# VectorE's masking of the forward diagonal score blocks, moved ahead of the last six operations of its pair

## The reference, cut to what matters

```python
p = p + (quad_shift(p, grid[0], grid[1]) - p) * mu
r, k, v, g, wl_f, wl_b, al_f, al_b = split_cols(p, RWKV_SIZES)
kk = to_heads(k * k_k, RWKV_HEADS).astype(jnp.float32)
kk = kk * lax.rsqrt(jnp.maximum(jnp.sum(jnp.square(kk), -1, keepdims=True), 1e-24))

def direction(w_lr, w0, ww2, a_lr, a0, wa2):
    w = jnp.exp(-RWKV_DECAY_SCALE * jax.nn.sigmoid((w0 + jnp.tanh(w_lr) @ ww2).astype(jnp.float32)))
    a = jax.nn.sigmoid(a0 + a_lr @ wa2)
    kh = to_heads(k * (1.0 + (a - 1.0) * k_a), RWKV_HEADS)
    bonus = jnp.sum(rh * kh * rk, -1, keepdims=True) * vh
    return (rh, to_heads(w, RWKV_HEADS), kh, vh, -kk, kk * ah), bonus
```

## Time and profile before

| | |
|---|---|
| median of 3 runs | 2932.02 us (2931.72 to 2933.52) |
| profiled execution, its span from first to last instruction | 2938.5 us |
| TensorE busy | 2522.4 us, 86% |
| VectorE busy | 1628.9 us, 55% |
| ScalarE, GpSimd busy | 918.9 us, 788.3 us |
| mean granted TensorE clock | 0.916 of full |

### The profile page before, as it was taken

The page is one execution under the profiler, slowest core; times in us unless marked ns, Lnnn a source line. Parts: engine busy times, 40 slices in busy tenths (PEclk is TensorE's granted clock), DMA queues, the critical chain, the costliest instruction groups (busy, mean ns, idle before and its releaser), DMA issues. The chain is left out here.

```text
span 2938.5 us, 56618 instructions
## 1 busy us (share of the span) xinstructions
PE 2522.4 (86%) x24270; PEld 2141.8 (73%) x24270; DVE 1628.9 (55%) x2534; ACT 918.9 (31%) x1488; POOL 788.3 (27%) x745
## 2 busy tenths in 40 slices
PE   6899898996898985676777999999689999996986
PEld 2577675675877874555566888878589999996765
DVE  3037787554356546685485566566546656564333
ACT  2113243231232334563203323333343334340310
POOL 1111111115756742111313222222122222121521
PEclk8899998998899997678898999999889999998998
DMA  7612445555343324120562444443634343412621
GB/s 267 239 52 84 136 134 145 149 154 162 86 112 95 95 76 117 25 73 17 174 147 76 154 164 156 165 163 141 226 120 164 117 159 109 158 58 71 204 90 60
DMA packets 338281, 374.11 MB, mean 127 GB/s; under 512 B 111279, under 2 KB 274742, under 8 KB 335470
## 3 DMA queue, kind: packets, MB, share of 16 engines
q1 hardware_dynamic: 337024, 367.15, 39.0%
q10 hardware_dynamic: 1006, 3.33, 0.3%
HBM read 230.60 MB, written 139.82 MB: 126 GB/s over the span
## 5 line engine op out<-in xcount | busy, mean ns | idle before, releaser
L3321 PE MATMUL PS<-V_hi,weights_hi 128*128 128x258 f32 x832 | 237.9, 286 | 10.4 <-DVE H L3532 6.9
L469 PE MATMUL PS<-hT_hi,w_in_hi 128*128 128x512 f32 (+1 forms) x640 | 239.5, 374 | 4.7 <-DVE q_out L3120 4.7
L469 PE MATMUL PS<-h_hi,w_in_hi 128*128 128x512 f32 (+1 forms) x624 | 233.1, 374 | 8.2 <-issue 4.6
L3322 PE MATMUL PS<-V_lo,weights_hi 128*128 128x258 f32 x832 | 236.8, 285 | 0.0
L471 PE MATMUL PS<-hT_hi,w_in_lo 128*128 128x512 f32 (+1 forms) x640 | 236.2, 369 | 0.0
L470 PE MATMUL PS<-hT_lo,w_in_hi 128*128 128x512 f32 (+1 forms) x640 | 236.1, 369 | 0.0
L3323 PE MATMUL PS<-V_hi,weights_lo 128*128 128x258 f32 x832 | 235.7, 283 | 0.0
L3429 POOL TENSOR_TENSOR weights_lo<-weights,weights_hi 128x1664 fp32r<-128x1664 f32 x32 | 122.0, 3812 | 412.4 <-ACT weights_hi L3381 412.4
L470 PE MATMUL PS<-h_lo,w_in_hi 128*128 128x512 f32 (+1 forms) x624 | 228.1, 366 | 0.0
L471 PE MATMUL PS<-h_hi,w_in_lo 128*128 128x512 f32 (+1 forms) x624 | 227.3, 364 | 0.0
L3293 PE MATMUL PS<-Q_hi,K_hi 128*128 128x256 f32 x640 | 184.2, 288 | 30.5 <-DMA K_lo<-kl_d 14.8
(11 more groups left out here) (462 smaller groups left out, 6378.3 us busy)
## 6 DMA issues: line engine op xcount, KB each, us to landing
chunk_in<-in_d SPq DMA_DIRECT2D x40, 512.0 KB, 3.5
w_in<-in_e_w_in_dram SPq DMA_DIRECT2D x30, 512.0 KB, 5.0
xnew<-in_o_w_in_dram SPq DMA_DIRECT2D x30, 512.0 KB, 6.2
in_d<-xnat SPq DMA_DIRECT2D x20, 640.0 KB, 6.1
modw<-in_mod_w_dram SPq DMA_DIRECT2D x12, 1024.0 KB, 9.5
xnat<-in_mod_w_dram SPq DMA_DIRECT2D x8, 1536.0 KB, 7.3
v_d<-xnew SPq DMA_DIRECT2D x16, 640.0 KB, 3.0
kh_d<-k_hi SPq DMA_DIRECT2D x16, 640.0 KB, 2.9
```

Source lines behind the costliest of these rows:

```text
L469: pe.matmul(PS[:, bank + off // 512, 0:n], wh[:, k], hh[:, k, t], start=(k == 0), stop=False)
L3321: pe.matmul(out, wh, VH[:, j, q], start=(j == seen[0]), stop=False)
L3322: pe.matmul(out, wh, VL[:, j, q], start=False, stop=False)
```

## The change

The call `blocks(p, 0)` moves from the end of VectorE's row for k = 4 to the place right behind L1067.

```diff
--- before.py
+++ after.py
@@ -1065,6 +1065,7 @@
                         dve.wait_ge(ready[1], 4 * p + 1)
                         link(dve.tensor_tensor(kk, kk, kt[1], ALU.mult))
                         dve.tensor_tensor(kk, kk, aa[1], ALU.mult).then_inc(ready[1], 1)
+                        blocks(p, 0)
                         dve.wait_ge(ready[1], 4 * p + 2)
                         link(dve.tensor_scalar(aa[1], aa[1], col(p, J_KA), ka1[:, p:p + 1], ALU.mult, ALU.add))
                         dve.tensor_tensor(aa[1], K, aa[1], ALU.mult).then_inc(s["kh_ok"], 1)
@@ -1074,7 +1075,6 @@
                         dve.wait_ge(ready[0], 4 * p + 4)
                         link(dve.tensor_tensor(khs, khs, aa[1], ALU.add))
                         dve.scalar_tensor_tensor(khs, R, col(p, J_RK), khs, ALU.mult, ALU.mult).then_inc(s["rk_ok"], 1)
-                        blocks(p, 0)
 
                 for n in range(last + 1):
                     prep(n)
```

## The result

The changed kernel takes **2909.64 us** (median of 4 runs, 2908.69 to 2915.1) against 2932.77 us for the kernel before (4 runs, 2931.72 to 2936.89): a ratio of 0.9921, 95% interval 0.9908 to 0.9934. That is 23.1 us less, where the prediction had 18.5 (2932.0 to 2913.5 us). The profiled execution after took 2909.42 us; its first to last instruction is a span of 2907.6 us, at a mean granted clock of 0.922.

What follows compares the result with a forecast made beforehand. TensorE was taken to bound the stage, stalled 18.0 us by late masks. Pairs 0, 1 and 2 give 4.5 + 10.4 + 3.6 = 18.5 us, so 2932.0 becomes 2913.5 us; range 2905.5 to 2924.5.

Steps and rivals of the forecast that it cites:

- three stalls: TensorE's waits before `w0` of pairs 1, 2 and 3, for the masks' PSUM banks: 4.45, 10.25 and 3.34 us, all to go.
- a gain of nothing: Rival, chance 0.09: block stores too slow, so pair 1 gives nothing and pairs 0 and 2 leave 8.1 us: 2923.9 us.
- no stop of 3.5 us was added: Rival, chance 0.08: three backward products each meet a 3.5 us stop and 3.1 us of low clock, no change: 2933 us.
- the rest of the program did not lengthen: Rival, chance 0.03: the shift of later work meets the clock's grants badly, costing 28.7 us, slower: 2942 us.
- Pair 0: 4.5 predicted: Before the next pair's `w0`: the 4.45 us stall goes entirely, with +0.1 us for the clock.
- The clock term: From `w0` to `a0`, clock and pieces behind each stall: -0.96 to +2.11, +1.03 to +4.10 and -0.76 to +2.31 us.
- tile 11: Place of a `w1` product held by no mask, 12.61 us including ScalarE's 1.26 us wait, used as the slow clock bound.
- Pair 1: 10.4 predicted: Stall and clock would give 11.3 to 14.4 us, but block stores delay the backward mask and bonus, capping it at 10.5.
- Pair 2: 3.6 predicted: Before the next pair's `w0`: the 3.34 us stall goes, with +0.3 us for the clock.
- Pair 3: nothing predicted: No `w0` follows, so no gain; later VectorE operations and stores were taken as covered and costed at nothing.
- the cover that I counted on: In pair 3, stores landing near 661 us and the bonus following at 665.84 us were to leave some 4 us.
- The held mask: In pair 1, GpSimd might hold the moved mask, making TensorE wait about 2 us; taken as zero, kept in the range.

Runs made afterwards that it cites:

- moved_all: The changed kernel itself, run again on the chip where its parts were timed: 2912.93 us against 2933.39 us for the kernel before.
- before_two: The kernel before, masks at the old place, with a separate block buffer and semaphore for each direction: 2934.26 us, ratio 0.9998.
- keep3: The changed kernel with the forward masks moved in pairs 0, 1 and 2 only, pair 3's left at the old place: 2915.96 us.
- warm: The changed kernel with a one-column sigmoid on ScalarE ahead of its wait for TensorE, loading the table early: 2905.05 us.
- warm_two: The changed kernel with both the early one-column sigmoid on ScalarE and two block buffers: 2903.85 us, and 2902.1 us when repeated.

## Why the prediction was right

The mechanism of the forecast held: three stalls removed, with the gain in pair 1 ended by the stores of the block buffer. The measured 23.1 us lie inside the range and 4.6 us above the forecast of 18.5. The rivals fell: the stores did end pair 1, but not at a gain of nothing, no stop of 3.5 us was added, and the rest of the program did not lengthen in this trace (2254.1 to 2248.3 us; in moved_all it was 2257.0). Of the 5.2 us by which the stage gained more than the forecast, 1.9 us (pair 0) repeat in every trace, while 2.1 us (pair 2) and most of the 3.15 us behind pair 3 differ from trace to trace with the clock and with TensorE's unnamed stop. That part of the size was luck, for or against; the medians of the two comparisons on record differ too, 23.1 and 20.5 us.

- **Pair 0: 4.5 predicted, 6.38 measured.** The stall's 4.45 us went in full. The clock term gave 0.51 us, between the bounds, where I had chosen 0.1. What I left out is tile 11: `w1` to `a1` took 12.61 us before and 11.15 us after, 1.46 us. I had used this product as a bound, as if the change left it alone. 4.45 + 0.51 + 1.46 = 6.42 us. The two places belong together: with the masks at the old place, before_two had 13.26 us at `w0` and 11.15 at `w1`, 24.4 us in all where before had 11.65 + 12.61 = 24.3, and the kernel after has 22.3. The low clock behind the stall falls on the one or the other.
- **Pair 1: 10.4 predicted, 8.97 measured.** The start of the bonus, counted from the pair's forward block product, moved from 476.14 - 434.81 = 41.33 us to 457.96 - 426.98 = 30.98 us: 10.35 us. The working by the stores, the backward mask and the bonus held to 0.1 us, its parts less well: `kh_ok` came 0.2 us later within the pair, not 1.0, in part because L1070 lost 1.6 us beside GpSimd (2.49 against 0.94 us) where the 2.0 us of before were expected again, and the issue of the row on SyncE's queue took 14.9 us where it had taken 14.3. The term was mis-sized at its end: behind the wait of 2.35 us the bonus ran in 3.97 us, not 2.57, and these 1.40 us were in no sum. The granted clock from 456 to 462 us was 0.72 of full, a mean of the two levels of 1.2 and 2.4 GHz, after TensorE had stood still for the 2.35 us.
- **Pair 2: 3.6 predicted, 5.70 measured.** The stall of 3.34 us went. The clock term gave 2.33 us (11.85 to 9.52), the fast end of my bounds, -0.76 to +2.31, where I took a third from the slow end. It is not steady: in moved_all, the same code, this place took 12.67 us, past the slow end of the bounds, and pair 2 gained 2.7 us. The windows of the kernel after (columns as before) show why a single row could not decide it: the two places have the same form and the same wait of 1.26 us, and yet

```profile
437.00:449.00 12.00, 10.74 (x33) 6.93 (x33) 11.86 (x9) 3.02 (x4) 1.87 (x1) 0.86 0.90 253
533.00:543.00 10.00, 8.74 (x33) 5.51 (x33) 3.86 (x2) 3.02 (x4) 0.96 (x1) 1.00 1.07 318
```

  the granted clock behind it was 0.86 in pair 1, so in part 1.2 GHz, and 1.00, 2.4 GHz, in pair 2. With a third from the slow end I was between the two executions; one nearer row does not tell which comes.
- **Pair 3: nothing predicted, 3.15 us measured**, from the last forward block product to the bonus (25.23 to 22.08). The stop after the product lost 2.92 us (3.48 to 0.56), the matmuls behind it 1.50 us (14.40 to 12.90, the low clock behind the long stop), and the cover that I counted on, "some 4 us", was used up: TensorE came to the bonus 4.3 us earlier (3.15 + the 1.13 that it waited), and the backward mask came 639.55 - 619.11 = 20.4 us after the forward one, where my times gave 661 - 641.6 = 19.4 us. The step that failed is the sentence that the bonus follows "at 665.84 us": it held a stop, and a low clock behind it, that did not come again. "If pair 3's bonus waits" was one of my signs of being wrong, and it came true, with 1.13 us. It did not cost the forecast because more than it had gone ahead of it; keep3 shows only that stop and wait can nearly cancel.
- **The held mask: zero, as taken.** See below.
- **The signs.** The 18.0 us are gone; the wait of L872 in pair 1 is 2.35 us (1 to 4 predicted); VectorE's wait in pair 3 is 14.43 us (some 14); the bonus of pair 0 starts at 360.14 (near 362), of pair 1 at 457.96 (461) and of pair 3 at 640.19 (647), ahead of the forecast by about the terms above and by 1.45 us that the stage began earlier. From the bonus of pair 3 to the next phase TensorE took 0.5 us longer (18.55 to 19.07).

6.38 + 8.97 + 5.70 + 3.15 - 0.52 = 23.68 us, the stage. The median moved by 23.1 us.

## What to carry to other kernels

When products share PSUM banks in a fixed order, read who takes the one before out, and move that step up in its engine's row to where its data are ready. Here it cost that engine nothing that showed, and each stall went by itself. Then compute where the next wait ends the gain (here a single buffer whose stores stand behind larger ones), and count covers with TensorE's new, earlier time, including the stops that the change removes. A short wait among small products is priced with the clock behind it, and in bounds: 1.26 us of ScalarE cost 1.26 us in one place and 2.9 us in others. And repeat a trace before reading a few microseconds out of it.

## What the runs showed of the hardware

**The mask is not held by GpSimd, its neighbour is.** GpSimd's timeline in the kernel after, pair 1:

```profile
436.52 2.35 POOL L980 TENSOR_TENSOR w_in_lo<-w_in,w_in_hi 128x1024 fp32r<-128x1024 f32 x1 [14.46 <-ACT w_in_hi L911]
```

The two masks ran from 436.27 to 437.15 us, so that the second lay inside it, and took 0.88 us as elsewhere. In warm the first backward mask of pair 1 began 1.7 us into GpSimd's operation (446.57 against 444.86 us), and the two took 0.89 us. L1070 began inside it and took 2.49 us, against 0.94 us in pair 3. The Trainium skill (SBUF — State Buffer, Who interferes with whom) says that a VectorE instruction with at most one SBUF input outside the two-port modes does not contend with GpSimd. The traces agree, with 0.88 and 0.89 us.

**A low clock follows short waits, and not every time.** Of the three `w0` places, each with its 1.26 us wait, `a0` followed after 11.14, 11.09 and 9.52 us; in moved_all, the same code, after 11.15, 11.15 and 12.67 us. With the wait taken away (warm) it was 8.27, 8.27 and 8.26 us, and 8.26 to 8.27 us in both traces of warm_two: the scatter went with the wait.

**TensorE's unnamed stop goes with transfers in one place and not in others.** Behind pair 3's forward product it was 0.56 us at a transfer share of 0.02 and 3.48 us at 1.10. Beside pair 2's, at 0.97, there was none; inside pair 0's it was 2.96 us after the change and 3.04 us before, at a share of some 0.5. The cause stays open.
